# Two-layer diffusion trunk: long convolution in two PSUM banks of its own, in turn with the mLSTM's steps; adaLN tiles ahead of the out-projection's

## The reference

```python
mod = (jax.nn.silu(cond) @ w_ada + b_ada)[..., None, :]   # 6 x 1024 columns a layer

def long_conv(z, h):                                      # circular convolution by FFT
    k = jnp.concatenate([h[0], jnp.zeros_like(h[0][:1]), h[1][:0:-1]], axis=0)
    zf, kf = jnp.fft.rfft(z, n=2 * L, axis=1), jnp.fft.rfft(k, n=2 * L, axis=0)
    return jnp.fft.irfft(zf * kf[None], n=2 * L, axis=1)[:, :L]

def hyena_mixer(u, ...):
    u = short_conv3(u, conv_w)
    v, x1, x2 = jnp.split(u, 3, axis=-1)
    z = x1 * (long_conv(v, h[0]) + d[0] * v)              # r = 0
    return x2 * (long_conv(z, h[1]) + d[1] * z)           # r = 1

def even_mixer(xm, w_in, ...):
    u = xm @ w_in
    y_hy = hyena_mixer(u[..., :3 * HY_W], ...)
    h, C, n, m = mlstm_bidir(q, k, v, gates, C0, n0, m0)  # C, n, m are outputs too
    h = rmsnorm(h, ml_norm_g) * sigmoid(o)
    return concatenate([y_hy, h]) @ w_out, C, n, m
```

## Time and profile before

| | us |
|---|---|
| median of three runs | 1507.32 (1502.74 to 1511.62) |
| the profiled execution: device time | 1515.6 |
| the profiled execution: span from first to last instruction | 1513.8 |
| TensorE busy | 1375.6 (91%) |
| VectorE busy | 1044.8 (69%) |
| ScalarE busy | 818.2 (54%) |

### The profile page before, as it was taken

The page is one execution under the profiler, slowest core; times in us unless marked ns, Lnnn a source line. Parts: engine busy times, 40 slices in busy tenths (PEclk is TensorE's granted clock), DMA queues, the critical chain, the costliest instruction groups (busy, mean ns, idle before and its releaser), DMA issues.

```text
span 1513.8 us, 16384 instructions
## 1 busy us (share of the span) xinstructions
PE 1375.6 (91%) x6400; PEld 1075.4 (71%) x6400; DVE 1044.8 (69%) x1015; ACT 818.2 (54%) x908; POOL 25.4 (2%) x44
## 2 busy tenths in 40 slices
PE   5788897579999987878999999999999999999995
PEld 1565463268888766767888888888888888888783
DVE  0563336453554576455789889899898998988985
ACT  1433122144344456344777777777777777777772
POOL 3000000000000020000000000000000000000000
PEclk9899998699999998687999999999999999999997
DMA  9878767253555541242999999999999999999990
GB/s 330 286 271 312 251 220 261 90 188 128 178 194 185 177 127 32 84 143 80 329 364 356 355 337 346 364 361 351 335 343 362 360 354 342 346 352 368 351 347 30
DMA packets 288117, 400.94 MB, mean 265 GB/s; under 512 B 15974, under 2 KB 224065, under 8 KB 287969
## 3 DMA queue, kind: packets, MB, share of 16 engines
q1 hardware_dynamic: 282048, 391.23, 76.0%
q0 software_dynamic: 1792, 4.28, 0.9%
q10 hardware_dynamic: 4192, 4.31, 0.8%
HBM read 397.93 MB, written 1.84 MB: 264 GB/s over the span
## 4 chain that ended last, share of the span: by engine, by line
PE 78%; DVE 4%; ACT 2%; DMA 2%; issue 1%; SPq 0%; DVEq 0%
PE bank L1740 76%; DMA raw<-in_w_ada 2%; PE bank L2097 2%; ACT arena L1027 1%; PE bank L2196 0%; SPq L602 0%; DVE w_lo L501 0%; ACT xn L777 0%; PE bank L1791 0%; ACT w_hi L494 0%; ACT arena L1037 0%; ACT Gb L796 0%; DVE arena L1730 0%; DVE x L1505 0%; DVE arena L1504 0%
## 5 line engine op out<-in xcount | busy, mean ns | idle before, releaser
L501 DVE TENSOR_TENSOR w_lo<-raw,w_hi 128x2048 fp32r<-128x2048 f32 (+1 forms) x238 | 543.3, 2283 | 164.2 <-ACT w_hi L494 162.8
L494 ACT CAST w_hi<-raw 128x2048 fp32r<-128x2048 f32 (+1 forms) x238 | 451.7, 1898 | 173.0 <-PE bank L1740 101.4
L1740 PE MATMUL bank<-w_hi,x_hi 128*128 128x512 f32 x1072 | 437.9, 409 | 24.5 <-issue 15.1
L1740 PE MATMUL bank<-w_lo,x_hi 128*128 128x512 f32 x1072 | 426.6, 398 | 0.0
L1740 PE MATMUL bank<-w_hi,x_lo 128*128 128x512 f32 x1072 | 423.3, 395 | 0.0
L1740 PEld LDWEIGHTS bank<-w_hi,x_hi 128*128 128x128 f32 x1072 | 204.3, 191 | 73.6 <-issue 27.7
L1740 PEld LDWEIGHTS bank<-w_hi,x_lo 128*128 128x128 f32 x1072 | 204.7, 191 | 47.3
L1740 PEld LDWEIGHTS bank<-w_lo,x_hi 128*128 128x128 f32 x1072 | 205.0, 191 | 39.4 <-issue 0.2
L501 DVE TENSOR_TENSOR w_lo<-arena,w_hi 128x2048 fp32r<-128x2048 f32 x88 | 201.7, 2292 | 36.9 <-ACT w_hi L494 36.9
L494 ACT CAST w_hi<-arena 128x2048 fp32r<-128x2048 f32 x88 | 168.0, 1909 | 27.8 <-PE bank L1740 27.8
L1740 PE MATMUL bank<-w_hi,g_hi 128*128 128x512 f32 x440 | 173.9, 395 | 1.8 <-DVE g_lo L1461 1.8
(11 more groups left out here) (285 smaller groups left out, 983.4 us busy)
## 6 DMA issues: line engine op xcount, KB each, us to landing
raw<-in_moe_w SPq DMA_DIRECT2D x352, 512.0 KB, 5.5
arena<-in_moe_w SPq DMA_DIRECT2D x176, 512.0 KB, 5.5
raw<-in_w_ada SPq DMA_DIRECT2D x96, 512.0 KB, 6.9
raw<-in_ff_w SPq DMA_DIRECT2D x66, 512.0 KB, 4.4
raw<-in_ev_w_in SPq DMA_DIRECT2D x28, 512.0 KB, 7.0
raw<-in_at_w_qkv SPq DMA_DIRECT2D x12, 512.0 KB, 4.5
raw<-in_ev_w_out SPq DMA_DIRECT2D x8, 512.0 KB, 8.1
raw<-in_at_w_out SPq DMA_DIRECT2D x8, 512.0 KB, 4.5
```

The lines of the kernel that those rows point to most:

```text
L494: nc.scalar.copy(w_hi[:, t % SPL, c], place[:, c]).then_inc(hi_ok, 1)
L501: nc.vector.tensor_tensor(w_lo[:, t % SPL, c], raw_slot(n)[0][:, c], w_hi[:, t % SPL, c].bitcast(F32), ALU.subtract).then_inc(lo_ok, 1)
L1740: return pe.matmul(out, lhsT, rhs, start=start, stop=stop)
```

## The change

The edit does five things.

- The long convolution goes through banks 6 and 7 alone, one step n = 2r + g after another: `fft(n)`, `fft_product(n)`, `inverse_fft(n)`, `hyena_gate(n)`. Its products lie in `zre`/`zim`. The mLSTM's numerators that used banks 6 and 7 go to banks 0 and 1.
- These steps stand between the mLSTM's, from right after `ada(17)`. `ada(22)` and `ada(23)` follow `fft(3)`, with the last inverse behind them.
- In `stream` all adaLN tiles come ahead of OUT[0] to OUT[3]. ScalarE's `stage_rows(2)` stands behind `high(OUT[0])` only, and `low(OUT[0])` comes ahead of VectorE's share of `take_turned(1)`, `low(OUT[1])` behind it.
- `gate_rows(0)` moves from ahead of the out-projection to behind its first tile.
- Early, `ada_half(8)` and `ada_half(9)` move ahead of the filter's first layer, and `low(IN[5])` moves ahead of the scans, `low(IN[6])` ahead of `normalised(1)`.

```diff
-        for m in range(19, 22):
+        for m in range(19, 24):
             put_ada(m)
         OUT = []
-        for i, t in enumerate(halves(a["ev_w_out"][0], 0) + halves(a["ev_w_out"][0], 512)):
+        for t in halves(a["ev_w_out"][0], 0) + halves(a["ev_w_out"][0], 512):
             OUT.append(len(stream))
             stream.append(t)
             is_ada.append(False)
-            if i in (1, 2):
-                put_ada(21 + i)
...
             high(OUT[0])
+            stage_rows(2)
             high(OUT[1])
+            take_turned(1, None)
             high(OUT[2])
-            stage_rows(2)
-            take_turned(1, None)
             gate_rows_out(0)
...
             low(IN[4])
+            low(IN[5])
             eng.wait_ge(g_f, 1)
...
             normalised(0)
-            low(IN[5])
+            low(IN[6])
             normalised(1)
-            low(IN[6])
...
+            def fft_product(n):
+
+                r = n // 2
+                A, B, Dd = spec[:, r, 0, :], spec[:, r, 1, :], spec[:, r, 2, :]
+                re, im = zre[n % 2], zim[n % 2]
+                eng.wait_ge(fz_mm, n + 1)
+                if n >= 2:
+                    eng.wait_ge(iz_mm, n - 1)
+                v_.tensor_tensor(re, bank[6][:, :], A, ALU.mult)
+                link(v_.tensor_tensor(ztmp, bank[7][:, :], B, ALU.mult))
+                link(v_.tensor_tensor(re, re, ztmp, ALU.subtract))
+                v_.tensor_tensor(im, bank[6][:, :], B, ALU.mult)
+                link(v_.tensor_tensor(ztmp, bank[7][:, :], Dd, ALU.mult))
+                link(v_.tensor_tensor(im, im, ztmp, ALU.add))
+                eng.sem_inc(fz_ok, 1)
+
+            def hyena_gate(n):
+
+                r, g = n // 2, n % 2
+                eng.wait_ge(iz_mm, n + 1)
+                dst = xn[:, g, 0:HW] if r else u[:, g, 0:HW]
+                v_.tensor_tensor(dst, u[:, g, HW * (1 + r):HW * (2 + r)], bank[6][:, :], ALU.mult).then_inc(iz_ok, 1)
...
+            fft_product(0)
             eng.wait_ge(den_mm, 1)
...
+            hyena_gate(0)
+            head_rows(0)
+            head_rows(1)
+            fft_product(1)
+            head_rows(2)
+            eng.wait_ge(kr_ok, 1)
...
+            hyena_gate(1)
+            head_rows(3)
+            fft_product(2)
             link(v_.tensor_tensor(sq, hall, hall, ALU.mult))
             v_.tensor_reduce(sml[:, 32:40], sq.rearrange("p g (h n) -> p (g h) n", h=NH), AX, ALU.add
                              ).then_inc(hs_q, 1)
+            hyena_gate(2)
+            fft_product(3)
             eng.wait_ge(ld_mg, 16)
...
+            hyena_gate(3)
             eng.wait_ge(iz_ok, 4)
...
+            low(OUT[0])
             take_turned(1, None)
-            eng.wait_ge(iz_mm, 4)
+            low(OUT[1])
             eng.wait_ge(ada_col, 3)
...
+            ada_half(8)
+            ada_half(9)
             eng.wait_ge(modc_ok, 1)
...
             proj(0, IN[0], 16)
-            ada_half(8)
-            ada_half(9)
...
             ada(17)
+            eng.wait_ge(st_ok, 4)
+            fft(0)
...
             mixer_half(13, 1)
+            inverse_fft(0)
...
             ada(18)
+            fft(1)
...
             ada_cols(1)
+            inverse_fft(1)
...
             ada(20)
+            fft(2)
...
+            inverse_fft(2)
             ada(21)
+            fft(3)
+            ada(22)
+            ada(23)
+            inverse_fft(3)
             eng.wait_ge(cs_t, 3)
```

More of the change, by code:

```diff
@@ L959, in _ @@
             high(OUT[0])
+            stage_rows(2)
             high(OUT[1])
+            take_turned(1, None)
             high(OUT[2])
-            stage_rows(2)
-            take_turned(1, None)
             gate_rows_out(0)
-            for n in (OUT[3], FF0, FF0 + 1):
-                high(n)
+            high(OUT[3])
+            high(FF0)
+            high(FF0 + 1)
             norm_root(1)
@@ L1224, in add_projection @@
                 low(out[3])
-                low(ahead[0])
+                if s:
+                    low(ahead[0])
+                eng.wait_ge(gbt, 4 * (s + 1))
                 for i in range(4):
@@ L1231, in add_projection @@
                     if i == 1:
+                        if s == 0:
+                            low(ahead[0])
                         low(ahead[1])
@@ L1394, in _ @@
             hall = xn[:, :, HW:2 * HW]
-            sq = hyT[0][:, 0:2, :]
+            sq = hyT0[:, 0:2, :]
+            hyena_gate(0)
[4 more added lines that the diff above has]
+            eng.wait_ge(kr_ok, 1)
+            for d in range(NDIR):
+                ins = v_.scalar_tensor_tensor(kw[:, d], heads(bank[0][:, :]), HD ** -0.5,
+                                              bc(cols[:, 3, 32 * d:32 * d + 4], HD), ALU.mult, ALU.mult)
+            ins.then_inc(kw_ok, 1)
+            hyena_gate(1)
+            head_rows(3)
+            fft_product(2)
             link(v_.tensor_tensor(sq, hall, hall, ALU.mult))
@@ L1992, in _ @@
                     eng.wait_ge(ld_C[0], 16)
+                    eng.wait_ge(tj_t, 15)
                 for h in range(NH):
@@ L2002, in _ @@
             ins.then_inc(nu_ok, 1)
+            eng.wait_ge(nu_t, 2)
+            for h in range(NH):
+                ins = pe.transpose(bank[0][:, P * h:P * h + P], kT[:, h, 0:T], ident)
+            ins.then_inc(kr_ok, 1)
             ada(19)
@@ L2005, in _ @@
             ada_cols(1)
-            eng.wait_ge(nu_t, 2)
-            for h in range(NH):
-                ins = pe.transpose(bank[6][:, P * h:P * h + P], kT[:, h, 0:T], ident)
-            ins.then_inc(kr_ok, 1)
+            inverse_fft(1)
             eng.wait_ge(ld_C[1], 16)
@@ L2063, in out_proj @@
                         pair_half(1 if n0 == 0 else 4, w0[2 * i + h], h, [out_bank(n + g) for g in range(G)], ready)
-            wait_inputs(1, 1)
-            gate_rows(0)
+                        if n == 0 and h == 0:
+                            wait_inputs(1, 1)
+                            gate_rows(0)
             out_proj(0, OUT)
```

70 lines of the change are left out of this document (21 added, 49 removed).

## The result

The changed kernel takes 1498.3 us in the median of 20 runs (1489.6 to 1506.3), the kernel before 1511.4 (1501.2 to 1522.6, 20 runs beside them). The ratio of the times is 0.9925, 95% interval 0.9905 to 0.9946: 11 us faster by the ratio, 13 by the two medians, where 21.7 were forecast. The time lies in the range (1476 to 1499), at its upper end, and in size it lies between the two values of rival (b), -15 and -10. The profiled execution took 1496.2 us, its span is 1494.4.

A forecast was written before the change was run, and what follows sets the result against it. It took a 62.6 us chain of waits before the out-projection, with neither TensorE nor DMA saturated, as the bound. -23.9 + 2.2 = -21.7 made the profiled 1515.6 us 1493.9 and the median 1507.3 1485.6; range 1476 to 1499.

The forecast's parts named there:

- gate_rows(0): Behind the out-projection's first tile: its 4.30 us wait goes, its 16 matmuls take 3.73 us instead of 6.12.
- (b): Load side stays the bound, early move costs 5: -15, 1492 us; with OUT[0] worse still, -10, 1497; chance 0.19.
- 23b: Second half tile for ada(23): there at 264.7 us, between 260 (no effect of the stores) and 266.8 (all of it).
- The convolution's order: Interleaved TensorE stretch: convolution costs the path seven transforms, 13 us, ahead of 254.4; waits for product(2) may be 0.6 us.
- the landing of the loads behind the stores: Loads ahead of the out-projection: 23b at 264.7 us, OUT[0] at 264.3, so the copy waits for 23b only.
- the late bound: Stores' full effect on the loads: 23b at 266.8 us, OUT[0] held 14 us to 269.4; 20 us saved.
- The rule that it named beside this: Writes below 512 B cause read-modify-writes, so out_n's 1024 single floats disturb their neighbours; gives 266.8 us for 23b.
- The wait for OUT[0] ahead of the copy: ScalarE's copy for stage_rows(2): if stores hold OUT[0] 14 us, copy done at 272, ada_cols(2) begins 1.7 us later.
- The early moves: Ahead of the mLSTM's scans: adaLN halves gain 0, VectorE's low parts cost 2.2 us; bounds -1 and +5, by TensorE's clock.
- (c): Behind 326 us: saved time comes back because the feed-forward's first tiles are not there; 0 to -5, about 1505; chance 0.05.
- (d): TensorE's clock stays at the low level through the interleaved part: +16, 1523 us, slower; chance 0.03.
- -23.9: Saved up to the out-projection's end, 302.2 us instead of 326.1; about 28 with the early bounds, 20 with the late.

The follow-up runs named there:

- stores late: Changed kernel with both state stores (out_C, out_n) issued after the split of OUT[3]: 1485.9 us, ratio to the kernel before 0.9864.
- VectorE's order undone: Changed kernel with low(IN[5]) back behind normalised(0) and low(IN[6]) behind normalised(1), ada_half(8) and (9) left early: ratio to the kernel before 0.9894.
- adaLN halves undone: Changed kernel with only ada_half(8) and ada_half(9) put back behind proj(0), VectorE's early order kept: ratio to the kernel before 0.9903.
- both undone: Changed kernel with low(IN[5]), low(IN[6]), ada_half(8) and ada_half(9) all back in their old places: ratio to the kernel before 0.9885.
- only out_C is late: Changed kernel with only out_C's store issued after the split of OUT[3], out_n's store left in place: 1495.4 us, ratio to the kernel before 0.9913.
- the copy first: Against the kernel with both early moves undone and both stores late: stage_rows(2) ahead of the cast of OUT[0]; 1481.4 us, ratio to the kernel before 0.9818.

## Why the prediction missed

On the trace's clock, the forecast's steps counted from the end of ada(17), which it had at 208.9 and the trace has at 213.39:

| step | forecast | measured | stores late |
|---|---|---|---|
| numerators begin | 16.2 | 17.6 | 17.6 |
| ada(22) done | 47.4 | 48.4 | 48.5 |
| 23b begins | 55.8 | 59.6 | 52.6 |
| ada_cols(2) begins | 61.4 | 66.7 | 57.8 |
| out-projection begins | 67.6 | 72.6 | 62.4 |
| out-projection ends | 93.3 | 100.3 | 88.0 |

- **The convolution's order: right.** Seven transforms in the path, product(2) waited for by 0.81 (forecast 0.6), a product of 4.06 (4.1), no wait for 22a and 22b. The 1.4 us too many are the second part of the denominators, which took 3.51 us behind fft(0) instead of 1.93: it ran at the low clock.
- **The step that failed is the landing of the loads behind the stores, OUT[0]'s above all.** The forecast gave OUT[0] the 8.9 us from issue to cast of OUT[2], a load with nothing else in the queue, so that "the copy waits for 23b only". It took 16.6 us (15.3 to 15.8 in the three other executions with both stores in place), beyond the 14 of the late bound, and the path went through OUT[0]: cast, copy, ada_cols(2). With both stores late it took 7.6. The four executions, from the end of ada(17):

| kernel | 23b begins | OUT[0] is cast | ada_cols(2) begins | out-projection begins | ends |
|---|---|---|---|---|---|
| forecast | 55.8 | 55.4 | 61.4 | 67.6 | 93.3 |
| changed | 59.6 | 64.2 | 66.7 | 72.6 | 100.3 |
| VectorE's order undone | 56.2 | 63.0 | 65.5 | 71.4 | 97.1 |
| adaLN halves undone | 55.8 | 63.5 | 66.0 | 71.9 | 100.0 |
| both undone | 56.5 | 63.4 | 65.9 | 71.8 | 97.4 |

- **23b.** In the changed kernel it came 3.8 us later than I had it and 1.7 later than my late bound (whose 14.2 us are 13.9 by its own rows). In the three others it came within 0.7 us of the forecast, and still the out-projection began 3.8 to 4.3 us late, since OUT[0] did. So a right time for 23b alone would not have saved the forecast. That it fits there is in part luck: the value was chosen by the number of tiles ahead, while 22b's 14 us were no property of the queue but a stall behind out_n. The kernel before shows it, with 22b on its way until 256.79, in a view that the prediction does not use (DMA, 245 to 258 us, slices of 0.325 us):

```profile
GB/s 400 386 389 383 397 394 391 400 408 377 399 403 381 396 383 372 390 379 195 92 21 7 0 0 0 0 0 0 0 44 50 57 0 0 0 13 32 50 50 19
```

The rate was back at 259.3 us, 18 us behind the issue of out_n, and in the changed kernel at 274, 17 us behind it. My text had the reason for doubt in it ("no row separates out_n from out_C") and still priced the two loads one by one. The rule that it named beside this gave the late bound; for 23b that is nearer in the changed kernel, and farther in the three others. For OUT[0] it points the right way.

- **The wait for OUT[0] ahead of the copy** was priced at 1.7 us in the late bound; it cost 2.36 behind the late 23b, and 4.69 to 5.21 in the three executions in which 23b came in time. The turn took 3.65 us, as forecast, and the first tile 7.8 instead of 5.5: 2.3 more, by the clock. Which of the waits lowers the clock is not shown: the tile took 5.7 us behind waits of 4.52 and 4.77, and 8.1 behind 3.37 and 5.21.
- **gate_rows(0)** at 3.73, as forecast, with no wait ahead of it.
- **The early moves: the mechanism was right, the size was off.** The term was +2.2; the two profiled executions give 4.5, the means of eleven and five executions 5.9, beyond the upper bound of 5. low(IN[5]) was no 0.9 us earlier, since its tile came at 94.78 instead of 93.87; low(IN[6]) ran at 109.85 (forecast 109.0). Behind the wait of 3.91 the tile ran partly at the low clock, as the upper bound had it, and this one is among the six of twelve in which it did.
- **Rivals.** (b), 23b and OUT[0] at or behind the late bounds and an early loss near 5, is what happened in the changed kernel, -12.4 in the trace: I gave it 0.19, too little with the trace's own 14 us for it. (c): nothing came back behind the out-projection, whose end is followed by 1181 us here and by 1188 in the kernel before, where the clock was lower (0.82 against 0.90 from 547 to 647 us). (d): the granted clock from 208 to 256 us, through all the alternating groups, was 0.93 (row below), so small idles did not bring it down. The Trainium skill's account of such cycling ("TensorE: Matmul & The Clock Gate", section "A second HAM failure mode: psum-queue depth-cycling") is not what this stretch shows, in which no wait is longer than 0.81 us.

```profile
208.00:256.00 48.00, 46.40 (x261) 30.64 (x259) 27.64 (x43) 5.19 (x8) 0.56 (x1) 0.93 0.59 203
```

In the sum: -23.9 became -16.9 (+1.0 up to ada(22), +6.0 by the stall and the clock behind it), and +2.2 became +4.5: -12.4 in the profiled execution, -11 by the ratio, -13 by the medians. Taken over all executions, S is 98.7 in the mean of the four above instead of 93.3, and the early loss 5.9 instead of 2.2: my estimate from these is -21.7 + 5.4 + 3.7 = -12.6.

## What to carry to other kernels

Look at every small store by the size of its contiguous pieces, not by its bytes: 4 KB in single floats held all weight loads for 6 to 9 us, and a transpose of 0.3 us or a later place took that away. When loads are moved to a new place, ask which stores now stand ahead of them, look at the rate while an oddly late load is on its way, and apply what is found to every load behind the store, not to one. And when a low part or a copy is moved ahead on an engine that then has to wait for its data, price what is queued behind it also with a lower clock, as one of two cases, and not only with the wait. A single execution can mislead on such a price; here eleven said 5.9 us where one said 4.5.

## What was unexpected of the hardware

- 128 writes of 4 bytes slowed the reads of other buffers to 0 to 51 GB/s for 6.6 us; 1024 of them did so (7 to 55 GB/s) for 8.4; 128 writes of 32 bytes did not. With 1024 of them the stalled packets took 1.4 us each instead of 0.083.
- The stall outlasts the writes: in the kernel in which only out_C is late, the last of them was followed by 8 us without one, while the reads crawled.
- The length of the waits ahead did not tell at which clock the 24 matmuls of the out-projection's first tile run: 5.7 us behind a wait of 9.94 (only out_C late), 7.3 us behind none longer than 2.58 (the copy first), 7.8 us behind 7.64 and 2.36 (the changed kernel).
